# Moving all weight residuals of the first mixer to VectorE, and one more channel tile of convolution sums to GpSimd

## The reference

```python
def conv_attention_mixer(h, w_in, w_out, dw_w, dw_b, ln_g, ln_b, qn_g, kn_g, sinks):
    z = h @ w_in
    a, gate, q, k, v = jnp.split(z, [s1, s2, s3, s4], axis=-1)
    u = a * jax.nn.sigmoid(gate)
    u = causal_depthwise_conv(u, dw_w) + dw_b        # 31 taps, 1024 channels
    u = jax.nn.silu(layer_norm(u, ln_g, ln_b))
    q = rms_norm(q.reshape(b, t, N_Q_HEADS, HEAD_DIM), qn_g)
    k = rms_norm(k.reshape(b, t, N_KV_HEADS, HEAD_DIM), kn_g)
    o = banded_sink_attention(q, k, v, sinks)
    return jnp.concatenate([u, o], axis=-1) @ w_out
```

## Time and profile before

| | |
|---|---|
| median of 3 runs (lowest, highest) | 2104.96 us (2104.64, 2107.4) |
| the profiled execution's own time | 2106.28 us |
| its span | 2104.5 us |
| mean granted TensorE clock | 0.998 of full |
| TensorE busy | 2065.0 us, 98% of the span |
| VectorE, ScalarE, GpSimd busy | 1355.9, 1099.2, 557.8 us |

### The profile page before, as it was taken

One profiled execution on the slowest core, in us unless ns is written; L12 is line 12 of the kernel. 1 busy time (PEld: TensorE's weight loads), 2 busy tenths in 40 slices (PEclk: granted clock), 3 DMA queues, 4 the chain that ended last, 5 costly groups with the idle time before them and its releaser, 6 DMA issues.

```text
span 2104.5 us, 24220 instructions
## 1 busy us (share of the span) xinstructions
PE 2065.0 (98%) x9582; PEld 1718.7 (82%) x9582; DVE 1355.9 (64%) x1377; ACT 1099.2 (52%) x1260; POOL 557.8 (27%) x293
## 2 busy tenths in 40 slices
PE   8999999999999999999999999999999999999999
PEld 6888777888888888888888888878888888888887
DVE  4786878955888358873442333478738984389832
ACT  6677565644555445554544444555545554455542
POOL 3676730022000420014454444410040003400033
PEclk9999999999999999999999999999999999999999
DMA  7543454556565565645566665556466555655554
GB/s 235 165 131 111 141 207 166 177 178 222 180 213 177 190 210 196 232 158 177 176 202 190 190 187 190 172 196 243 154 214 218 176 184 190 240 179 187 189 191 161
DMA packets 208273, 394.29 MB, mean 187 GB/s; under 512 B 11296, under 2 KB 21536, under 8 KB 208160
## 3 DMA queue, kind: packets, MB, share of 16 engines
q1 hardware_dynamic: 207872, 392.21, 55.4%
q10 hardware_dynamic: 288, 0.53, 0.1%
HBM read 390.60 MB, written 2.10 MB: 187 GB/s over the span
## 4 chain that ended last, share of the span: by engine, by line
PE 89%; issue 4%; DVE 4%; ACT 2%; POOL 1%; DMA 0%; DVEq 0%; SPq 0%; ACTq 0%; POOLq 0%
PE pair L636 14%; PE pair L638 14%; PE pair L637 14%; PE pair L711 9%; PE pair L713 9%; PE pair L712 9%; PE pair L696 5%; PE pair L698 5%; PE pair L697 5%; PE tbank L726 2%; DVE w_lo L1535 1%; DVE pair L1688 1%; ACT w_hi L1110 1%; POOL cv L602 1%; DMA w_raw<-in_w_in 0%
## 5 line engine op out<-in xcount | busy, mean ns | idle before, releaser
L1110 ACT ACTIVATE w_hi<-w_raw 128x1024 fp32r<-128x1024 f32 x608 | 641.9, 1059 | 649.8 <-PE pair L638 407.1
L590 POOL TENSOR_TENSOR w_lo<-w_raw,w_hi 128x1024 fp32r<-128x1024 f32 x192 | 475.4, 2477 | 1531.7 <-ACT w_hi L1110 1531.6
L1535 DVE TENSOR_TENSOR w_lo<-w_raw,w_hi 128x1024 fp32r<-128x1024 f32 x416 | 534.2, 1285 | 499.0 <-ACT w_hi L1110 498.3
L711 PE MATMUL pair<-w_hi,xT_hi 128*128 128x512 f32 x880 | 342.6, 389 | 2.8 <-DVE w_lo L1535 2.8
L713 PE MATMUL pair<-w_hi,xT_lo 128*128 128x512 f32 x880 | 342.4, 389 | 0.0
L712 PE MATMUL pair<-w_lo,xT_hi 128*128 128x512 f32 x880 | 342.4, 389 | 0.0
L1110 ACT ACTIVATE w_hi<-s_raw 128x1536 fp32r<-128x1536 f32 x154 | 229.2, 1488 | 165.5 <-PE pair L713 120.9
L1535 DVE TENSOR_TENSOR w_lo<-s_raw,w_hi 128x1536 fp32r<-128x1536 f32 x154 | 269.9, 1762 | 60.2 <-ACT w_hi L1110 60.0
L636 PE MATMUL pair<-w_hi,yT_hi 128*128 128x512 f32 x704 | 274.6, 390 | 0.0
L638 PE MATMUL pair<-w_hi,yT_lo 128*128 128x512 f32 x704 | 274.0, 389 | 0.0
L637 PE MATMUL pair<-w_lo,yT_hi 128*128 128x512 f32 x704 | 273.9, 389 | 0.0
(11 more groups left out here) (179 smaller groups left out, 2613.9 us busy)
## 6 DMA issues: line engine op xcount, KB each, us to landing
w_raw<-in_w_down SPq DMA_DIRECT2D x176, 512.0 KB, 4.2
w_raw<-in_w_up SPq DMA_DIRECT2D x110, 512.0 KB, 6.4
w_raw<-in_w_gate SPq DMA_DIRECT2D x110, 512.0 KB, 3.7
w_raw<-in_sc_in SPq DMA_DIRECT2D x96, 512.0 KB, 3.8
s_raw<-in_w_gate SPq DMA_DIRECT2D x44, 768.0 KB, 8.0
s_raw<-in_w_up SPq DMA_DIRECT2D x44, 768.0 KB, 8.0
w_raw<-in_w_in SPq DMA_DIRECT2D x52, 512.0 KB, 3.9
w_raw<-in_w_out SPq DMA_DIRECT2D x32, 512.0 KB, 3.5
```

The costliest lines, as they stand in the source:

```text
L590: nc.gpsimd.tensor_tensor(w_lo[at], raw(o), w_hi[at].bitcast(F32), ALU.subtract).then_inc(w_lo_pool, 1)
L711: nc.tensor.matmul(b, x_hi(k, t), w_hi[:, r, kk, :], start=(first[t] and kk == 0), stop=False)
L1110: nc.scalar.activation(w_hi[:, o % RING, tiles_of(o), :], raw(o), ACT.Copy).then_inc(w_hi_ready, 1)
L1535: nc.vector.tensor_tensor(w_lo[at], raw(o), w_hi[at].bitcast(F32), ALU.subtract).then_inc(w_lo_dve, 1)
```

## The change

In the first mixer all low parts are made on VectorE (40 slots move there: the odd ones of 1 to 67 and of 73 to 83). GpSimd, free of them, adds tiles 0, 1 and 2; VectorE keeps tile 3 alone of the first four, so 31 taps move. ACT makes 3 products a slot in slots 21 to 51 in place of 2, and GpSimd runs its whole list of additions in one go. The portions of VectorE's taps between the low parts are dealt out anew; `lows_and_taps` now makes two low parts and then the taps. From the first feed-forward network on, nothing is changed.

```diff
-    def job(self, name, pair, k_tiles, adds=False, slot_k=SLOT_K, on_vector=False):
+    def job(self, name, pair, k_tiles, adds=False, slot_k=SLOT_K):
...
-            self.operand(True, self.slots % 2 == 1 and not on_vector)
+            self.operand(True, self.slots % 2 == 1 and self.shared)   # False until the first plan_sums
...
-        pool_taps = [(c, k) for k in range(TAPS) for c in (0, 1)] + [(4, k) for k in range(SHARE)]
+        pool_taps = [(c, k) for k in range(TAPS) for c in (0, 1, 2)] + [(4, k) for k in range(SHARE)]
-        dve_taps = [(c, k) for k in range(TAPS) for c in (2, 3)]
+        dve_taps = [(3, k) for k in range(TAPS)]
...
-            first = max(0, min(2 * (s - FIRST_TAP + 1), 2 * TAPS))
+            first = max(0, min(3 * (s - FIRST_TAP + 1), 3 * TAPS))
...
-            for s in range(1, first_ffn, 2):
-                if ON_POOL[s]:
-                    low(s)
-                add_taps(products_by(s - 2), products_by(s))
+            add_taps(0, len(pool_taps))
...
-                lows(max(2 * b, 1), 2 * b + 1)
+                lows(max(2 * b, 1), 2 * b + 2)
...
-                    lows(s, s + 1)
+                    lows(s - 1, s + 1)
                     taps = conv_taps(taps, min(taps + each, end))
...
-            taps = lows_and_taps(kv0 + 6, q00 + 4, 0, 4, U0_TAPS)
+            taps = lows_and_taps(kv0 + 6, q00 + 4, 0, 1, U0_TAPS)
             key_sums()
-            taps = lows_and_taps(q00 + 4, q00 + 6, taps, 6, U0_TAPS)
+            taps = lows_and_taps(q00 + 4, q00 + 6, taps, 2, U0_TAPS)
             key_norms()
-            taps = lows_and_taps(q00 + 6, q10 + 4, taps, 7, U0_TAPS)
+            taps = lows_and_taps(q00 + 6, q10 + 4, taps, 2, U0_TAPS)
             query_sums(0)
-            taps = lows_and_taps(q10 + 4, q10 + 6, taps, 2, U0_TAPS)
+            taps = lows_and_taps(q10 + 4, q10 + 6, taps, 1, U0_TAPS)
             query_norms(0)
-            taps = lows_and_taps(q10 + 6, q10 + 10, taps, 6, U0_TAPS)
+            taps = lows_and_taps(q10 + 6, q10 + 10, taps, 1, U0_TAPS)
             score_rows(0)
-            taps = lows_and_taps(q10 + 10, q10 + 12, taps, 3, U0_TAPS)
+            taps = lows_and_taps(q10 + 10, q10 + 12, taps, 1, U0_TAPS)
...
-            lows(ao0 + 16, ao0 + 17)
+            lows(ao0 + 15, ao0 + 17)
             conv_taps(taps, ALL_TAPS)
```

More of the change, by code:

```diff
@@ L74, in __init__ @@
         self.units = {}
+        self.shared = False
     def operand(self, loaded, on_pool):
@@ L205, in encoder_kernel @@
     for nb in range(NJ):
-        plan.job(("conv_out", nb), OUT_PAIRS[nb], KD // 2, on_vector=(nb == 0))
+        plan.job(("conv_out", nb), OUT_PAIRS[nb], KD // 2)
     def plan_sums(norm):
@@ L222, in encoder_kernel @@
     plan_sums(1)
+    plan.shared = True
     def down_pairs(ch):
@@ L366, in encoder_kernel @@
         ALL_TAPS = len(dve_taps)
-        acc_place = {2: 0, 3: 1, 5: 0, 6: 1, 7: 0}
+        acc_place = {3: 1, 5: 0, 6: 1, 7: 0}
         FIRST_TAP, SECOND_TAPS = JOB["kv"][0] + 5, JOB[("g1", 0)][0] + 13
         def products_by(s):
-            first = max(0, min(2 * (s - FIRST_TAP + 1), 2 * TAPS))
-            return first + max(0, min(2 * (s - SECOND_TAPS + 1), len(pool_taps) - 2 * TAPS))
+            first = max(0, min(3 * (s - FIRST_TAP + 1), 3 * TAPS))
+            return first + max(0, min(2 * (s - SECOND_TAPS + 1), len(pool_taps) - 3 * TAPS))
         def starts_sum(c, k):
@@ L1679, in conv_taps @@
                     if k == 0:
-                        if n >= 2:
+                        if n >= 1:
                             dve.wait_ge(tap_done, n)
@@ L1823, in _ @@
             multiply_pair("a0")
-            lows(kv0 + 4, kv0 + 6)
+            lows(kv0 + 4, kv0 + 5)
             u_copied(("u", 0, 0), ("u", 0, 1))
-            taps = lows_and_taps(kv0 + 6, q00 + 4, 0, 4, U0_TAPS)
+            taps = lows_and_taps(kv0 + 6, q00 + 4, 0, 1, U0_TAPS)
             key_sums()
-            taps = lows_and_taps(q00 + 4, q00 + 6, taps, 6, U0_TAPS)
+            taps = lows_and_taps(q00 + 4, q00 + 6, taps, 2, U0_TAPS)
             key_norms()
-            taps = lows_and_taps(q00 + 6, q10 + 4, taps, 7, U0_TAPS)
+            taps = lows_and_taps(q00 + 6, q10 + 4, taps, 2, U0_TAPS)
             query_sums(0)
-            taps = lows_and_taps(q10 + 4, q10 + 6, taps, 2, U0_TAPS)
+            taps = lows_and_taps(q10 + 4, q10 + 6, taps, 1, U0_TAPS)
             query_norms(0)
-            taps = lows_and_taps(q10 + 6, q10 + 10, taps, 6, U0_TAPS)
+            taps = lows_and_taps(q10 + 6, q10 + 10, taps, 1, U0_TAPS)
             score_rows(0)
-            taps = lows_and_taps(q10 + 10, q10 + 12, taps, 3, U0_TAPS)
+            taps = lows_and_taps(q10 + 10, q10 + 12, taps, 1, U0_TAPS)
             score_rows(1)
```

## The result

Measured side by side, 20 runs each, the changed kernel takes 2114.62 us (median) and the kernel before 2107.35 us; the ratio is 1.0034, 95% interval 1.0027 to 1.0042. So it is 7.3 us slower, where the forecast was 5.2 us. In these 20 runs the kernel before lies between 2104.3 and 2113.7, wider than its first three runs had shown, and its median is 2.4 us above theirs; that is more than half of the 4.4 us by which 2114.6 lies above the forecast time of 2110.2.

What follows compares the result with a forecast made beforehand. TensorE, busy 98%, bounds the kernel; VectorE bounds the stretch 223 to 257.1 us. Terms -0.2 + 6.6 + 0 - 1.2 = +5.2 on the median 2104.96 gave 2110.2 us; own range 2107 to 2114, whole range 2102.5 to 2115.5.

Steps and rivals of the forecast that it cites:

- the five low parts of slots 59 to 67: 223 to 257 us: added to a full VectorE, they cost +6.6 us, lower bound 5.0, upper bound 10.6.
- The rival by the port pair: 223 to 257 us: each moved low part also stops a GpSimd addition; cost up to 10.6 us, time 2114.
- the clock term: Slow clock after a 9 us pause before the channel means: could cost up to 2 us, taken as 0.
- slower still: Product buffers run short, ScalarE waits: 4 us, or as much by port or clock in the last stretch; 2114.5, chance 0.20.
- The attention part: 77 to 223 us: -1.7 + 1.6 + 2.3 - 2.4 = -0.2 us, between 4 won and 4 lost.
- 77 to 121.5: Shorter tap portions before query_norms and score_rows(0) win 1.7 us; the key_norms pause moves to slot 25, netting 0.
- Low part 39: 121.5 to 151.5 us: waits behind score_rows(1) and query_sums(1), ends a pause of 1 to 3 us; stretch +1.6.
- the gain of 1.4: Pause at 202.15 us: ScalarE's 1.8 us wait for GpSimd's additions goes, one more product costs 0.4: -1.4.
- At 219.47: Pause behind a small VectorE instruction held up by a GpSimd low part; chain begins 0.5 earlier: -1.0 us.
- 257 to 345: Low parts 81 and 82 made together on VectorE, 82 ready 1.2 us earlier: -1.2 us (0 to 2).
- Faster: GpSimd's long holds of VectorE slow the attention part; some 8 us of pauses go, sum -4.2: 2100.7, chance 0.13.
- No change: Added low parts fall into VectorE's waits also in the last stretch: some 2104, chance 0.17.

Runs made afterwards that it cites:

- e1: Changed kernel with the low parts of slots 59, 61, 63, 65 and 67 back on GpSimd: 2108.47 us, ratio 1.0002 to the kernel before.
- e2: Kernel before with only the low parts of slots 59, 61, 63, 65 and 67 moved to VectorE: 2115.27 us, ratio 1.004.
- e6: Changed kernel with 10 of VectorE's 56 taps of tiles 6 and 7 moved to GpSimd: 2116.02 us, ratio 1.0035 to the kernel before.
- e3: Changed kernel with 24 unread matmuls filling TensorE's pause before the last tap: 2111.29 us, ratio 1.0017 to the kernel before.
- e7: Changed kernel with unread matmuls filling four TensorE pauses (7, 11, 24 and 11 matmuls): 2109.08 us, ratio 1.0003 to the kernel before.
- e4: Changed kernel with tile 3's 31 taps dealt out anew, more of them earlier: 2112.59 us, ratio 1.0024 to the kernel before.
- e10: Kernel before with only the low parts of slots 65 and 67 moved to VectorE: 2112.78 us, ratio 1.0026.
- e9: Kernel before with unread matmuls filling three of its own TensorE pauses (5, 8 and 11 matmuls): 2108.55 us, ratio 1.0009.
- e8: Changed kernel with the edits of e1 and e4 and four pauses filled (7, 7, 8 and 11 matmuls): 2101.4 us, ratio 0.997 to the kernel before.
- e5: Changed kernel with the edits of e1 and e4 together: 2105.47 us, ratio 0.999 to the kernel before.

## Why the prediction came out as it did

**Right: where the time goes.** The prediction put +6.6 us on the five low parts of slots 59 to 67 and about nothing on the other 35. e1 and e2 show just that from both sides (1.0002 without them, 1.004 with them alone). Mis-sized a little: from TensorE's first `attn_out` matmul to the last means the profiled pair grew from 32.8 to 265.43 - 227.17 = 38.3, so 5.5 us, nearer to the lower bound 5.0 than to 6.6. Of the signs named, VectorE had no idle time in the 35 us before the last tap, as said; the pause for the last tap was 5.68 and not over 6, and with the 1.13 before it 6.8, where some 9 in all were forecast. Four of five pairs of low parts went at 1.17 to 1.20 each in the changed kernel (2.34 to 2.40 a pair); I had counted more delay by the additions than two a slot make. With three a slot, in e6, it came. The rival by the port pair, in which this stretch costs up to 10.6 and the time is 2114, hits the total for a wrong reason: in this stretch eight of ten low parts ran at full speed, so its term was not paid there. It is not refuted elsewhere: from 77 to 223 us, with three additions a slot, the 35 low parts took 1.44 us each and not 1.22.

**Wrong: the clock term, "I take 0".** The price was named (up to 2) and then left out, and only for one pause. e3 puts what the last pause alone costs through the clock at about 0.17% or 3.5 us; e7 puts all four places at 0.31% or 6.5 us, which includes what the clock took in the attention part. With 5.5 for 6.6 and 3.5 for 0 the prediction's own sum is -0.2 + 5.5 + 3.5 - 1.2 = 7.6, close to 7.3. That the forecast of 5.2 came near is in part luck: the last stretch was put 1.1 us too high and the clock at nothing. The absolute time, 2114.6, is above the forecast's own range (2107 to 2114) and at the 2114.5 of "slower still", which named the clock in the last stretch as one of its ways.

**The attention part, forecast at -0.2.** By e1 it is right as a sum within the interval (1.0002, 0.999 to 1.0013, with the -1.2 of the next stage in it). In the profiled pair it is not: the first `attn_out` matmul is 2.8 us later (227.17 for 224.33), with the low clock in it. The single pauses came as follows.

- 77 to 121.5, forecast -1.7: better, the score rows start 4.9 us earlier. key_norms' k_twice ended at 86.3, not 87.6, and the pause there is 1.25 in place of 1.84 and 1.01; slot 25 waits, as foreseen, but only for that long.
- Low part 39 ends a pause (0.70 at 136.29, below the 1 us named), and the banks of score_rows(1) one of 1.47 at 127.06: right in kind.
- The pause at 149.6 grew from 1.30 to 1.76; ScalarE's three products (1.29 us) stand right ahead of the copy that ends it, but in e1 and e6, with the same three products, it is 1.25 and 1.27, so the third product is not shown as its cause.
- The transposes of u came 2.3 later than before, where the prediction's terms up to there give 2.2; but that stretch itself lost 4.2 (from 1.9 ahead to 2.3 behind) and not 2.3, of which the low clock after 149.6 took about 1.7 more than in the kernel before. Their pause is 2.72 for 0.76.
- At 202 the gain of 1.4 did not show: the pause (206.31, 2.29) now ends with VectorE's heads_out(2), which stands behind 8 taps and a low part whose high part came at 199.4; the wait of ScalarE for additions is gone as forecast, and another stood behind it.
- At 219.47 the gain was 1.25 for 1.0.

Without the clock the part might have won, an estimate: the low stretches at 148 to 160 and 176 to 188 are worth 3.4 us each by the windows, the kernel before has 3.4 in all of 77 to 223, the changed one 8.5. The 5.1 more are at most time lost, against the 2.8 by which the part was later.

**257 to 345, forecast -1.2.** Right in its mechanism, and hidden by the clock: from the second x sums (VectorE's step after the second `conv_out` job; 311.40 for 299.70, 11.7 later) to the last x_split but one (the splitting of x for the feed-forward network; 323.87 for 313.23, 10.6 later) 1.1 us are won, as VectorE makes 81 and 82 in 2.36 us in place of waiting for GpSimd. Over the whole stretch the changed kernel is slower all the same, 83.0 us (265.43 to 348.45) for 80.7 (257.11 to 337.82), 2.1 of it before conv_out.

**The rivals.** "Faster" failed between 120 and 176 us, where the 5 us won until then were lost again. By the two traces the clock took some 1.7 of this and tile 3's portions about 0.9 (the pause of 2.72 is 1.82 in e4); the rest is not taken apart. "No change" failed, as VectorE had no waits to fill (41.0 busy of 42.4). Two low parts already cost (e10). "Slower still" by the product buffers did not come: ScalarE waited 0.6 us for additions in all (1.8 before), though GpSimd had 3 a slot:

```profile
L1219 ACT ACTIVATE products<-uT,cols 128x256 f32<-128x256 f32 x126 | 55.0, 497 | 0.6 <-POOL cv L604 0.6
```

**Readings and sums.** The earlier trace rows shows two pauses that ScalarE ended; the trace of the kernel before has four from 77 to 223 us (141.52, 151.49, 190.96, 202.15). The 1.15 us for each `k_twice` was a mean of unlike ones: the longest took 2.38 us and the shortest 0.81, beside GpSimd's low part from 86.17 to 88.62. Two of the rivals' times are off a little by their own terms: 2104.96 - 4.2 is 2100.8, and 2110.2 + 4 is 2114.2.

**What stays open.** The size of the clock's share. For the last stretch e3 gives 3.5 us by the ratios and 2.1 in the traces; the five low parts cost 0.32% or 6.7 us by e1, of which 5.5 are VectorE's, so this way only 1.2 are left for the clock. e1 itself loses the clock at 268, so the three do not measure quite the same. The same pause of 2.88 kept the clock in one profiled execution (before) and lost it in another (e1). e9 gained nothing while e8 gained 0.2% over e5 with nearly the same fills. The trace of e9 shows one part of it, the small step held up beside a low part of GpSimd, which e8 has no more in that place; that this is all of it is not shown.

## What to carry to other kernels

Ask of work that is moved not how much of it there is but how much falls where the receiving engine is never idle: here 35 of 40 low parts cost nothing that can be told and 5 cost everything. A split of the move by stretch is level with the kernel before (e1), and with better portions just faster than it (e5). A chain of dependent steps of one tile costs more per step (0.53 us) than two tiles in turn (0.39), so giving a partner tile away saves less than its count says. When an order by hand makes TensorE stand still longer, count the granted clock after the pause as well as the pause; filling the pause with matmuls that nobody reads can show that cost by itself (e3, e7). Look at the new trace before trusting it: in e9 the fill moved other engines' work and made a new pause.

## What the runs showed of the hardware

The granted clock fell to its lower level also after pauses shorter than the 2.55 us of the earlier trace rows: after those of 1.76 us (changed kernel), 1.82 (e4), 2.72 (changed kernel) and 2.88 (changed kernel, e1) it was 0.50 to 0.57 in the window of 4 us that holds the pause's end or in the next one. The Trainium skill, page "TensorE: Matmul & The Clock Gate", section "Part 1: The HAM clock gate (the "warmup" mystery)", has the array fall back to 1.2 GHz when it has been idle; these runs agree in kind. It is not the same in each execution: after the same 2.88 us pause the clock was 1.00 in the kernel before and 0.57 in e1, and after pauses of 1.84 (at 91.02) and 2.08 us (at 257.11) it was 1.00 in the kernel before. With the pauses filled the runs came together (e8: 1.0 us from the lowest to the highest of six runs; e5, the same without the fills: 4.1; kernel before beside it: 7.8); in the kernel before they did not (e9: 2106.97 to 2113.75).

Small VectorE instructions were held up beside GpSimd's low parts: of the four `k_twice` instructions of 128 columns in the kernel before, the longest took 2.38 us and the shortest 0.81, and `rden`, 8 columns, took 0.16 us in the kernel before and 2.32 in e9, where it began 0.1 us after a low part on GpSimd of 2.40.
